# A float32 encoder layer on one core: the 1024-wide part of the input projection as seven half-size products instead of eight

## The chip, the cores and the metric

The program runs on one core of one Trainium2 chip. The metric is the device time of one execution in microseconds (us). The engines have short names: PE is TensorE (matrix products), DVE is VectorE, ACT is ScalarE, POOL is GpSimd, and SP is the engine whose queue issues nearly all DMA transfers here. Each engine works through its own instructions in order; semaphores order the engines among each other.

## What is computed

One layer (DEPTH = 1) on x of shape 1024 x 1024, all float32:

```
h = rmsnorm(x, norm1_g)
z = h @ w_in + b_in          # columns: q 512, k 128, v 128 | mq 256, mk 256, mv 512, mo 512, gates 8
att = window_sink_attention(aq, ak, av, sinks)      # 16 chunks of 64 tokens, each sees 2 chunks
mq, mk = silu(causal_dwconv([mq, mk]))              # 4 taps
ml = sigmoid(mo) * mlstm_chunkwise(mq, mk, mv, mi, mf)
x += concat(rmsnorm(att), rmsnorm per head(ml)) @ w_out
x += conv_ffn(rmsnorm(x))                           # up, 3 taps, silu gate, down
return rmsnorm(x, final_g)
```

## The kernel before

**Precision.** Every float32 factor A is split into A_hi (ACT rounds it to the type fp32r) and A_lo = A - A_hi (DVE). A product is three matmuls: hi·hi, hi·lo, lo·hi. A 128x128 by 128x512 matmul is the unit of PE's work.

**The projection.** h stands transposed in `h_hi` and `h_lo` as 8 blocks of 128 rows (k) by 1024 tokens. PE first makes the gates and column tiles 1 to 3 (their weights are split early), then "block b" for b = 4 to 10, one column tile of 128 each: `z_block(b)` is 8 k x 3 x 2 halves = 48 matmuls. Weights of tile b go through a ring of three buffers: SP loads them (`load_tile`), ACT rounds (`weight_high`, L865 to L870), DVE subtracts (`weight_low`, L1393). `z_block(b)` waits for `weight_low(b)`. DVE then takes the bank out (`z_scale`), ACT adds the bias (`z_keep`).

The remaining 1024 columns, the output gate mo and the values mv, have tokens as rows. They are the "wide" part: 16 units `wide_unit(v)` of 24 matmuls, four passes of four units, each pass 512 columns x 512 tokens over all 8 k. A pass fills four PSUM banks, which DVE takes out (`wide_keep`: times rstd, plus bias) into `ml_gate` or `ml_v`.

**Beside the blocks.** The attention runs in steps n, two per block or pair of units from block 8 on. At the even steps PE holds `turn_probs(n-2)`, `attend`, `score(n)`, `score(n+1)`, `turn_probs(n-1)`. Between a score and its turn, DVE takes the maximum (`att_top`), ACT the exponentials (`att_exps`), DVE the reciprocal of the sum (`att_sum`), POOL multiplies (`att_p_scale`, L809). `turn_values` at the start of block 8 needs `z_keep(6)`, and the first score needs `att_v_keep`. The output weights are split as the wide ones are (`wo_high`, `wo_low`), one of 8 row tiles per block from DVE's and ACT's loop index 5 on (`WO_BLOCK`), written to memory by SP (`store_wo`) and read back before the output projection.

**What sets the order.** All of it is written out by hand: a loop over `b` on ACT and DVE does in iteration b what the PE needs for block b+1 and b+2 (`weight_high(b+2)`, `z_scale(b)`, step n of the attention, taps of the convolution, `wo_*`). SP has a loop over tile numbers n from 7; in iteration n it waits until tile n-3 is used, loads tile n and does what else is attached to n. POOL has the 16 `att_p_scale` with one `decay_keep` behind each pair. SBUF is an arena of 51 slots of 4 KB per partition, with many names to one slot over time.

## Time and profile before

| | us |
|---|---|
| median of 3 runs (994.88 to 996.3) | 995.81 |
| the profiled execution | 995.28 |
| its span, first to last instruction | 993.4 |
| PE busy | 985.9 |
| DVE busy | 737.9 |
| ACT busy | 514.2 |
| POOL busy | 54.1 |

The profiled execution lies 0.5 us under the median. The span is 1.9 us shorter than that execution's own time. Busy times add up the instructions of an engine; PE's matmuls overlap, so its busy share says that there is always one in flight and not that they start as closely as they can. How closely they do is read from the distance of two starts.

### The profile page before, as it was taken

The numbers are of one execution on the slowest core, as the hardware profiler recorded it, in microseconds if no ns is written. First come the engines' busy times: TensorE is split into PE (matmuls) and PEld (weight loads), VectorE is DVE, ScalarE is ACT, GpSimd is POOL, SyncE is SP. The second block draws the span as 40 slices with busy tenths as digits, with TensorE's granted clock in tenths as the row PEclk, the third lists the DMA queues.
The fourth block names the chain that finished last, engine by engine and source line by source line (L and its number), as shares of the span: only waits on it lengthen the run. The fifth ranks groups of instructions, "written<-read, shape, count | busy, mean of one in ns | idle before, by whom it ended". The sixth has DMA issues, their size and how long they took to land.

```text
span 993.4 us, 12933 instructions
## 1 busy us (share of the span) xinstructions
PE 985.9 (99%) x4713; PEld 809.4 (81%) x4713; DVE 737.9 (74%) x1149; ACT 514.2 (52%) x1010; POOL 54.1 (5%) x53
## 2 busy tenths in 40 slices
PE   9999999999999999999999999999999999999997
PEld 7788887778888888888888888888888888888886
DVE  4563767866555669997777778777776879996896
ACT  4663556667733236654454445545445534444573
POOL 1000323311300000000000000000000000000000
PEclk9999999999999999999999999999999999999999
DMA  9528655236422242342232232223223998035104
GB/s 337 199 79 231 218 193 191 85 101 239 151 85 85 85 143 69 106 128 63 85 107 64 82 94 79 64 90 101 64 86 123 393 345 325 1 122 190 38 1 170
DMA packets 96007, 134.43 MB, mean 135 GB/s; under 512 B 6332, under 2 KB 56636, under 8 KB 95944
## 3 DMA queue, kind: packets, MB, share of 16 engines
q1 hardware_dynamic: 95128, 132.98, 40.7%
q8 instruction: 38, 0.62, 0.3%
q10 hardware_dynamic: 720, 0.61, 0.2%
q0 software_dynamic: 96, 0.00, 0.1%
q14 instruction: 25, 0.20, 0.1%
HBM read 104.75 MB, written 28.35 MB: 134 GB/s over the span
## 4 chain that ended last, share of the span: by engine, by line
PE 95%; DVE 1%; issue 1%; ACT 1%; DMA 1%; POOL 0%; SPq 0%; ACTq 0%; POOLq 0%
PE pz L2141 8%; PE pz L2434 8%; PE pz L2436 8%; PE pz L2435 8%; PE pd L2434 6%; PE pd L2436 6%; PE pd L2435 6%; PE pd L2459 4%; PE pd L2460 4%; PE pd L2457 4%; PE pz L2459 3%; PE pz L2460 3%; PE pz L2457 3%; PE pd L2335 3%; PE pd L2337 3%; PE pd L2336 3%
## 5 line engine op out<-in xcount | busy, mean ns | idle before, releaser
L1181 ACT ACTIVATE ws_hi<-raw 128x512 fp32r<-128x512 f32 x88 | 52.9, 626 | 102.5 <-PE pz L2436 47.3
L2434 PE MATMUL pz<-ht_hi,ws_hi 128*128 128x512 f32 x240 | 93.5, 390 | 0.0
L2436 PE MATMUL pz<-ht_hi,ws_lo 128*128 128x512 f32 x240 | 93.4, 389 | 0.0
L2435 PE MATMUL pz<-ht_lo,ws_hi 128*128 128x512 f32 x240 | 93.4, 389 | 0.0
L2434 PE MATMUL pd<-ht_hi,ws_hi 128*128 128x512 f32 x200 | 77.9, 389 | 0.0
L2436 PE MATMUL pd<-ht_hi,ws_lo 128*128 128x512 f32 x200 | 77.8, 389 | 0.0
L2435 PE MATMUL pd<-ht_lo,ws_hi 128*128 128x512 f32 x200 | 77.8, 389 | 0.0
L1888 DVE SCALAR_TENSOR_TENSOR gate<-u,vec,gate 128x1023 f32<-128x1023 f32 (+1 forms) x44 | 56.5, 1283 | 19.4 <-ACT gate L1223 18.6
L1858 DVE TENSOR_TENSOR ws_lo<-raw,ws_hi 128x512 fp32r<-128x512 f32 x88 | 58.6, 686 | 0.7 <-ACT ws_hi L1181 0.7
L1888 DVE SCALAR_TENSOR_TENSOR lift<-u,vec,lift 128x1023 f32<-128x1023 f32 (+1 forms) x44 | 56.2, 1278 | 0.1
L1256 ACT ACTIVATE d_hi<-a 128x512 fp32r<-128x512 f32 x44 | 27.7, 630 | 54.6 <-PE pd L2460 25.0
L2434 PEld LDWEIGHTS pz<-ht_hi,ws_hi 128*128 128x128 f32 x240 | 45.1, 188 | 9.9 <-issue 0.7
L2436 PEld LDWEIGHTS pz<-ht_hi,ws_lo 128*128 128x128 f32 x240 | 45.1, 188 | 9.4
L2435 PEld LDWEIGHTS pz<-ht_lo,ws_hi 128*128 128x128 f32 x240 | 45.0, 188 | 9.3
L1393 DVE TENSOR_TENSOR w_lo<-w_raw,w_hi 128x1024 fp32r<-128x1024 f32 x23 | 28.1, 1222 | 31.6 <-ACT w_hi L869 31.6
L2457 PE MATMUL pd<-d_hi,d_hi 128*128 128x512 f32 x132 | 51.3, 389 | 0.0
L2459 PE MATMUL pd<-d_lo,d_hi 128*128 128x512 f32 x132 | 51.3, 389 | 0.0
L2460 PE MATMUL pd<-d_hi,d_lo 128*128 128x512 f32 x132 | 51.3, 389 | 0.0
L2457 PE MATMUL pz<-d_hi,d_hi 128*128 128x512 f32 x132 | 51.3, 389 | 0.0
L2459 PE MATMUL pz<-d_lo,d_hi 128*128 128x512 f32 x132 | 51.3, 389 | 0.0
L2460 PE MATMUL pz<-d_hi,d_lo 128*128 128x512 f32 x132 | 51.3, 389 | 0.0
L2335 PE MATMUL pd<-wo_hi,mix_hi 128*128 128x512 f32 x128 | 50.9, 397 | 0.4 <-DVE mix_lo L1730 0.4
(316 smaller groups left out, 2557.4 us busy)
## 6 DMA issues: line engine op xcount, KB each, us to landing
raw<-in_w_up SPq DMA_DIRECT2D x48, 512.0 KB, 5.1
b<-in_w_down SPq DMA_DIRECT2D x49, 256.0 KB, 6.9
act_rows<-gate SPq DMA_DIRECT2D x22, 512.0 KB, 2.6
a<-act_rows SPq DMA_DIRECT2D x44, 256.0 KB, 4.7
w_raw<-in_w_wide SPq DMA_DIRECT2D x16, 512.0 KB, 3.5
x_in<-in_x SPq DMA_DIRECT2D x8, 512.0 KB, 12.9
wo_hi_rows<-wo_new_hi SPq DMA_DIRECT2D x8, 512.0 KB, 5.6
wo_lo_rows<-wo_new_lo SPq DMA_DIRECT2D x8, 512.0 KB, 6.4
```

The costliest lines, as they stand in the source:

```text
L1181: nc.scalar.activation(ws_hi[m][:, :, :], summand(p, i), ACT.Copy).then_inc(s["ws_hi_made"], 1)
L1858: nc.vector.tensor_tensor(ws_lo[m][:, :, :], summand(p, i), ws_hi[m][:, :, :].bitcast(F32), ALU.subtract)\
L1888: nc.vector.scalar_tensor_tensor(out=dst[:, back:], in0=src[:, 0:S - back], scalar=w, in1=dst[:, back:], op0=ALU.mult, op1=ALU.add).then_i ...
L2141: ins = mm(dst[:, h * HALF:(h + 1) * HALF], w[:, c], h_part(part, k, h), start=first, stop=last)
L2335: mm(bank[4 + n % 4], mix_hi[u][:, k, :], wo_hi[:, k, c], start=k == 0, stop=False)
L2336: mm(bank[4 + n % 4], mix_hi[u][:, k, :], wo_lo[:, k, c], start=False, stop=False)
L2434: mm(dst, wh[:, k, :], xh[:, k, :], start=begins and k == 0, stop=False, skip_group_check=not begins)
L2435: mm(dst, wh[:, k, :], xl[:, k, :], start=False, stop=False, skip_group_check=not begins)
L2436: ins = mm(dst, wl[:, k, :], xh[:, k, :], start=False, stop=k == KH - 1, skip_group_check=not begins)
L2457: mm(dst, d_hi[m, 0][:, c], d_hi[m, 1][:, :], start=begins and k == 0, stop=False, skip_group_check=not begins)
L2459: mm(dst, d_hi[m, 0][:, c], d_lo[m, 1][:, :], start=False, stop=False, skip_group_check=not begins)
L2460: ins = mm(dst, d_lo[m, 0][:, c], d_hi[m, 1][:, :], start=False, stop=k == KT - 1, skip_group_check=not begins)
```

## The change

The wide product W·h is cut in halves of k and of tokens, and in its two groups of 512 columns, and done with seven products of half-size matrices instead of eight. For the seven, four combinations of the halves of h and four of the quarters of the weights are needed.

- `wide_unit`: 14 units in seven products of two (`WIDE_ORDER` = 2, 5, 3, 1, 6, 7, 4). A product covers 4 k. Products 2, 5 and 1 begin the four banks anew; 3, 6, 7 and 4 add onto what the product before them left there. Each product's four banks are taken out (with the bias, or for 1, 6 and 7 onto what `ml_v` or `ml_gate` already holds), so `wide_keep` runs 28 times and not 16, and each product waits for the taking out of the one before.
- The sums of h: `load_rows` reads two 128-row blocks of x transposed, `sum_scale` (ACT, two instructions of 128x1024) applies the gain, `add_sums` (POOL, four of 128x512) makes the four combinations, `sums_high` (ACT, 128x2048) and `sums_low` (DVE, 128x2048) split them, `store_sums` (SP, two transfers of 1 MB) writes them to memory; four times (kk = 0 to 3), in two buffers. `load_sums` reads a quarter back over `h_hi` and `h_lo` before products 5, 3, 6 and 7.
- The sums of the weights: `load_weights(q)` reads four tiles of 512 KB, `add_weights(q, step)` (POOL, 128x1024) makes four, `store_weights(q)` writes them; for q = 0 and 1. They come back through the ring of tiles.
- `WO_BLOCK` is 3 and not 5: the output weights are split two iterations sooner.
- The attention keeps two steps per block through the wide part; the last steps lie closer together. `inter` and `decay` rows are spread later on SP.

The core of the diff:

```diff
-WO_BLOCK = 5
+WO_BLOCK = 3
+WIDE_ORDER = (2, 5, 3, 1, 6, 7, 4)
+UNITS = 2 * len(WIDE_ORDER)
...
@@ SP
+            def load_rows(kk):
+                ...
+                    sp.wait_ge(sum_stored[m][0], sum_stored[m][1] + 32)
+                for j in range(2):
+                    k = kk + KH * j
+                    sp.dma_start(s_sum[m][:, j, :], x_t[k * P:(k + 1) * P, :]).then_inc(sum_loaded[m][0], 16)
+            def store_sums(kk):
+                sp.wait_ge(sum_split, 2 + kk)
+                for dst, src in ((s_hi_d, s_hi), (s_lo_d, s_lo)):
+                    sp.dma_start(dst[kk], ...).then_inc(sum_stored[kk % 2][0], 16)
...
+            load_rows(0)
+            load_wo(0)
+            load_wo(1)
+            load_rows(1)
             for n in range(7, LAST_BLOCK + 1 + UNITS):
+                load_tile(n)
                 if n == 7:
-                    load_wo(0)
-                    load_wo(1)
-                load_tile(n)
+                    turn_store(0)
+                    store_sums(0)
+                    load_rows(2)
+                    store_sums(1)
+                    load_rows(3)
...
+                if n == 9:
+                    turn_store(2)
+                    store_sums(2)
+                    store_sums(3)
+                    load_weights(0)
+                    load_weights(1)
...
@@ POOL
-            for n in range(NC):
+            for kk in range(KH):
+                add_sums(kk)
+            for step in range(4):
+                add_weights(0, step)
+            att_p_scale(0)
+            add_weights(1, 0)
+            att_p_scale(1)
+            for step in range(1, 4):
+                add_weights(1, step)
+            for n in range(2, NC):
                 att_p_scale(n)
@@ ACT, iteration b, at its end
+                    if b == 3:
+                        sum_scale(half)
+                    if b == 4:
+                        sums_high(half)
+                    if b == 5 and half == 1:
+                        sum_scale(2)
+                        sum_scale(3)
+                    if b == 6:
+                        sums_high(2 + half)
@@ DVE, iteration b, at its end
+                    if half == 1 and b in (4, 6):
+                        sums_low(b - 4)
+                        sums_low(b - 3)
@@ PE
-            for v in range(UNITS):   # 16 units of 24 matmuls
+            for v in range(UNITS):   # 14 units of 24 matmuls
```

ACT's order from iteration b = 3 on. The names are `w_hi` for the rounded weights of a tile (`w_raw1` holds tile 7, `w_raw2` tile 8), `wo_new_hi` for the output weights, `z` and `zq` for what `z_keep` writes. Before:

```order
L921 ACTIVATE row_c_66<-row_c_66 4x1024
L924 ACTIVATE row_a_64<-row_b_65 4x1024
L869 ACTIVATE w_hi1_266<-w_raw1_260 128x1024
L983 ACTIVATE wo_new_hi0_57<-wo_raw0_53,vec 128x1024
L905 ACTIVATE z_59<-z_59,vec 128x1024
L869 ACTIVATE w_hi0_265<-w_raw2_261 128x1024
```

The same stretch now, tile 7 and tile 8 again the third and the last of the weights:

```order
L1095 ACTIVATE s_sum1_268<-s_sum1_268,vec 128x1024 x2
L970 ACTIVATE w_hi0_265<-w_raw0_259 128x1024
L1006 ACTIVATE zq_60<-zq_60,vec 128x16x64
...
L1025 ACTIVATE row_a_64<-row_b_65 4x1024
L1084 ACTIVATE wo_new_hi1_58<-wo_raw1_54,vec 128x1024
L1106 ACTIVATE s_hi0_271<-s_sum0_267 128x2048
L1106 ACTIVATE s_hi1_272<-s_sum1_268 128x2048
L970 ACTIVATE w_hi1_266<-w_raw1_260 128x1024
...
L1084 ACTIVATE wo_new_hi0_57<-wo_raw0_53,vec 128x1024
L1095 ACTIVATE s_sum0_267<-s_sum0_267,vec 128x1024 x2
L1095 ACTIVATE s_sum1_268<-s_sum1_268,vec 128x1024 x2
L970 ACTIVATE w_hi0_265<-w_raw2_261 128x1024
```

One output split and two splits of sums stand ahead of tile 7, and an output split and two pairs of scalings, which need newly loaded rows, ahead of tile 8.

POOL's order at the first two steps of the attention. Before:

```order
L802 MEMSET row_a_64 36x1024
L803 MEMSET row_c_66 4x1024
L809 TENSOR_TENSOR probs_312<-probs_312,inv 128x4x64
L809 TENSOR_TENSOR probs_312<-probs_312,inv 128x512
L816 AFFINE_SELECT decay_319<-decay_319 128x4x128
L809 TENSOR_TENSOR probs_312<-probs_312,inv 128x512 x2
```

Now:

```order
L910 TENSOR_TENSOR t_raw0_0_273<-t_raw0_1_274,t_raw0_0_273 128x1024
L910 TENSOR_TENSOR t_raw0_1_274<-t_raw0_2_275,t_raw0_1_274 128x1024
L910 TENSOR_TENSOR t_raw0_2_275<-t_raw0_2_275,t_raw0_0_273 128x1024
L910 TENSOR_TENSOR t_raw0_3_276<-t_raw0_3_276,t_raw0_2_275 128x1024
L879 TENSOR_TENSOR probs_326<-probs_326,inv 128x4x64
L910 TENSOR_TENSOR t_raw1_0_277<-t_raw1_1_278,t_raw1_0_277 128x1024
L879 TENSOR_TENSOR probs_326<-probs_326,inv 128x512
```

The first multiplication of the attention stands behind the 16 sums of h and the four weight sums of the first half, the second behind one more.

SP's order between tile 7 and tile 8 now (before, the loads of both tiles stood next to each other):

```order
L521 DMA w_raw1_260<-in_w_tiles 128x1024 [waits z_done]
L594 DMA wo_hi_rows<-wo_new_hi0_57 128x1024 [waits wo_split]
...
L555 DMA s_hi_rows<-s_hi0_271 128x2048 [waits x_rstd]
L555 DMA s_lo_rows<-s_lo0_269 128x2048
L550 DMA s_sum0_267<-in_x_t 128x1024 [waits x_loaded1]
...
L555 DMA s_hi_rows<-s_hi1_272 128x2048 [waits x_rstd]
L555 DMA s_lo_rows<-s_lo1_270 128x2048
L550 DMA s_sum1_268<-in_x_t 128x1024 [waits x_half_loaded]
...
L521 DMA w_raw2_261<-in_w_tiles 128x1024 [waits z_done]
```

The load of tile 8 moved behind the landing of both stores of sums (`x_loaded1` and `x_half_loaded` count them).

## Rows read from the trace of the kernel before

**Rows 1.** The page, busy time by engine.
```profile
PE 985.9 (99%) x4713; PEld 809.4 (81%) x4713; DVE 737.9 (74%) x1149; ACT 514.2 (52%) x1010; POOL 54.1 (5%) x53
```
**Rows 2.** Windows: us, busy (count) of PE PEld DVE ACT POOL; granted clock, DMA.
```profile
43.00:77.30 34.30, 34.30 (x166) 28.35 (x164) 22.45 (x25) 21.64 (x20) 0.00 (x0) 1.00 0.44 113
...
128.80:238.50 109.70, 109.63 (x602) 87.57 (x601) 77.37 (x170) 73.29 (x215) 26.42 (x17) 1.00 0.47 159
```
**Rows 3.** Timeline of PE, second and last matmul of two wide units: start, length.
```profile
142.87 0.39 PE L2369 MATMUL pz<-w_lo,h_hi 128*128 128x512 f32 x1
...
153.31 0.39 PE L2370 MATMUL pz<-w_hi,h_lo 128*128 128x512 f32 x1
```
**Rows 4.** Chain of waits: start, us, what (blocks 4 to 6, 7, turn_values, second turn_probs).
```profile
43.06 32.64 PE pz L2141 x144
...
77.34 11.11 PE pz L2141 x48
88.45 0.87 PE pd L2177 x8
...
108.52 0.59 PE pd L2204 x4
```
**Rows 5.** Timeline of ACT, iterations 3 to 6: start, us, instruction.
```profile
54.05 3.23 ACT L905 ACTIVATE zq<-zq,vec 128x1024 f32<-128x1024 f32 x3
57.19 1.04 ACT L869 ACTIVATE w_hi<-w_raw 128x1024 fp32r<-128x1024 f32 x1
...
68.20 1.06 ACT L869 ACTIVATE w_hi<-w_raw 128x1024 fp32r<-128x1024 f32 x1
...
79.28 1.15 ACT L905 ACTIVATE z<-z,vec 128x1024 f32<-128x1024 f32 x1 [1.39 <-DVE z L1427]
```
**Rows 6.** Timeline of DVE, same stretch.
```profile
59.78 1.23 DVE L1393 TENSOR_TENSOR w_lo<-w_raw,w_hi 128x1024 fp32r<-128x1024 f32 x1
...
65.87 1.21 DVE L1477 TENSOR_TENSOR row_b<-row_b,row_d 4x1024 f32<-4x1024 f32 x1
...
69.36 1.23 DVE L1393 TENSOR_TENSOR w_lo<-w_raw,w_hi 128x1024 fp32r<-128x1024 f32 x1 [1.57 <-ACT w_hi L869]
```
**Rows 7.** Groups of instructions: busy us, mean ns of one, idle before.
```profile
L1181 ACT ACTIVATE ws_hi<-raw 128x512 fp32r<-128x512 f32 x88 | 52.9, 626 | 102.5 <-PE pz L2436 47.3
...
L1858 DVE TENSOR_TENSOR ws_lo<-raw,ws_hi 128x512 fp32r<-128x512 f32 x88 | 58.6, 686 | 0.7 <-ACT ws_hi L1181 0.7
...
L1393 DVE TENSOR_TENSOR w_lo<-w_raw,w_hi 128x1024 fp32r<-128x1024 f32 x23 | 28.1, 1222 | 31.6 <-ACT w_hi L869 31.6
```
**Rows 8.** Groups of POOL, all of the span.
```profile
L829 POOL TENSOR_TENSOR mixed<-ml_t,ml_gate 128x512 f32<-128x512 f32 x8 | 10.2, 1277 | 44.0 <-DVE ml_t L1703 43.9
```
**Rows 9.** Timelines of POOL and of DVE where both read SBUF.
```profile
111.83 1.99 POOL L809 TENSOR_TENSOR probs<-probs,inv 128x512 f32<-128x512 f32 x1 [3.32 <-DVE inv L1546]
...
160.78 1.04 POOL L809 TENSOR_TENSOR probs<-probs,inv 128x512 f32<-128x512 f32 x1 [5.83 <-DVE inv L1546]
...
111.67 1.25 DVE L1567 SCALAR_TENSOR_TENSOR wo_new_lo<-wo_raw,vec,wo_new_hi 128x1024 fp32r<-128x1024 f32 x1
112.84 2.06 DVE L1493 SCALAR_TENSOR_TENSOR qk_acc<-z,vec,qk_acc 128x1022 f32<-128x1022 f32 x1
118.58 1.25 DVE L1493 SCALAR_TENSOR_TENSOR qk_acc<-z,vec,qk_acc 128x1021 f32<-128x1021 f32 x1
```
**Rows 10.** DMA: SP's issues, KB each, us to landing (128 to 140 us; all).
```profile
wo_lo_rows<-wo_new_lo SPq DMA_DIRECT2D x1, 512.0 KB, 5.9
...
act_rows<-gate SPq DMA_DIRECT2D x22, 512.0 KB, 2.6
...
w_raw<-in_w_wide SPq DMA_DIRECT2D x16, 512.0 KB, 3.5
```
**Rows 11.** GB/s in 40 slices of 92 to 104 us.
```profile
GB/s 0 0 0 0 273 410 314 219 218 259 123 68 96 191 205 273 382 423 437 423 437 369 437 437 423 396 232 0 0 0 0 0 0 177 164 410 314 246 273 205
```
**Rows 12.** Timeline of PE, its first matmuls after standing idle.
```profile
1.39 4.21 PE L2098 MATMUL pd<-idle_data 128*128 128x512 f32 x9 [1.39 <-POOL idle_data L773]
```

More of the change, by code:

```diff
@@ L994, in _ @@
                 z_keep(b)
[L995 to L996 removed]
+            for b in range(FIRST, LAST_BLOCK + UNITS // 2):
+                if 0 <= att_step(b + 1, 0) - 2 < NC - 1:
                     att_p_keep(att_step(b + 1, 0) - 2)
@@ L1029, in _ @@
                             silu_qk(n // 16 * 2 + m)
+                    if n == NC + 1:
+                        for m in range(NC - 4, NC):
+                            att_square(m)
+                    for i in DECAYS.get(n, ()):
+                        decay_exp(i)
+                    if n == NC:
+                        att_p_keep(NC - 1)
+                    if n == NC + 2:
+                        for i in range(NT // 2):
+                            wide_gate(i)
             def ml_square(i):
@@ L1084, in _ @@
             ml_key(0)
-            for i in range(NT):
+            att_total_keep()
+            for i in range(NT // 2, NT):
                 wide_gate(i)
-            att_total_keep()
             att_root()
@@ L1615, in _, with sums_low @@
             z_scale(2)
-            for b in range(FIRST, ZT + 1):
+            def sums_low(kk):
+                m = kk % 2
+                dve.wait_ge(sum_hi_made, 2 + kk)
+                nc.vector.tensor_tensor(s_lo[m][:, :, :], s_sum[m][:, :, :], s_hi[m][:, :, :].bitcast(F32),
+                                        ALU.subtract).then_inc(sum_split, 1)
+            for b in range(FIRST, LAST_BLOCK + UNITS // 2):
                 for half in range(2):
@@ L1634, in _ @@
                         z_scale(b)
-                    for m in (n - 4, n - 3):
-                        if n % 2 == 0 and 0 <= m < NC:
-                            att_keep(m)
+                    if n % 2 == 0 or n == NC + 1:
+                        first = n - 4 if n <= NC else NC - 2
+                        for m in (first, first + 1):
+                            if 0 <= m < NC and n <= NC + 1:
+                                att_keep(m)
                     if 0 <= n < NC:
```

292 lines of the change are left out of this document (197 added, 95 removed).

## The prediction, made before the changed kernel ran

> **What bounds the kernel now.** I read the page's busy times first, then the windows, then the chain of waits, then each engine's timeline from 40 to 125 us. PE is busy 985.9 of 993.4 us [rows 1] and in the wide stretch 109.63 of 109.70 us at a granted clock of 1.00, its level of 2.4 GHz [rows 2]. From 43 to 128.8 us the chain of waits is PE alone [rows 4]. So the end is set by PE: matmuls taken away count in full, and so does every wait put before PE. What must be asked of each added step is how early its result was there before. Block 7 started at 77.34 us [rows 4]; its weights were rounded by ACT from 68.20 and finished by DVE at 69.36 + 1.23 = 70.6 [rows 5, 6], 6.7 us ahead. `turn_values` started at 88.45 [rows 4]; the `z_keep(6)` that it needs ended at 79.28 + 1.15 = 80.4 [rows 5], 8.0 us ahead. These two leads are all that the new work of iterations 3 to 6 may use.
>
> **What is removed.** Two of 16 wide units, 48 matmuls. 46 starts lie between the second and the last matmul of two units: (153.31 - 142.87) / 46 = 0.227 us [rows 3]. 48 x 0.227 = **10.9 us off**, all on PE.
>
> **What a new instruction costs.** ACT: 128x1024 takes 1.05 and 128x512 0.626 [rows 5, 7], so 128x2048 takes 1.05 + 2 x 0.43 = 1.9 us. DVE: 1.222 and 0.686 [rows 7], so 2.3 us for 2048. POOL: 1.28 for 512 [rows 8]; 1.04 is the least seen [rows 9]; for 1024 I take twice that, 2.1 to 2.5. DMA: 1 MB in two stores lands 5.9 us after the second issue [rows 10], so 6.4 after the first, which SP issues some 0.5 us sooner; the engines move at most about 0.41 MB per us over a few slices [rows 11], so 2 MB land in 6.4 + 2.5 = 8.9 us; the low bound takes 2.6 us for the first 512 KB [rows 10] and gives 2.6 + 3.8 = 6.4. A lone load of 512 KB takes 3.5 [rows 10]: 1 MB 4.5 at most.
>
> **Step 1, block 7.** ACT was busy with the gates until 54 and `z_keep` until 57.2, then rounded tile 6 [rows 5]. Now an output split and four scalings of 1.05 stand ahead of that: 5.3 us later, until 63.5. DVE finishes tile 6 at 64.8; block 6 starts at 43.06 + 2 x 10.88 = 64.8 [rows 4], just in time. Everything behind is late too: DVE's tile 6 started at 59.78 [rows 6] and now at 63.6, so the gate row that ended at 65.87 + 1.21 [rows 6] ends at 70.9, ACT's second gate exponential at 72.0, the second output split at 73.1, the two splits of sums at 76.9, tile 7 at 78.0. DVE: first low part 75.0 to 77.3, second to 79.5, tile 7 at 80.8. Block 7 starts 80.8 - 77.34 = 3.5 us late. That is the short end.
> The long end adds the collisions of POOL and DVE. A POOL multiplication of 128x512 took 1.04 us at 160.78, and 1.99 at 111.83, where DVE had begun a 1.25 us instruction at 111.67; DVE's next one, at 112.84, took 2.06 and its like 1.25 at 118.58 [rows 9]. The two take turns. POOL's eight additions start at 60.4, when the first scaling is done, in the midst of DVE's gate rows; three of them fall between rows that wait for each other: 3 x 1.28 = 3.8 us. Block 7 would start at 84.7, 7.3 late.
> The Trainium skill says so too: by its page "SBUF — State Buffer", section "SBUF: two separate sides", the port pair of DVE and GpSimd is an exclusive lock held for a whole instruction, against a DVE instruction with two SBUF inputs. By that rule the long end holds; without it the short one would. The trace agrees with the lock (1.99 against 1.04).
>
> **Step 2, block 8.** The first low part is done at T0 = 77.3 to 81.1. SP then stands in one file: store both parts (8.9; low 6.4), load the next rows, store the second pair behind them (3 MB, 11.4; low 8.9), load rows 3 (4.5; low 4.0), and only behind that tile 8. Sum 24.8, low 19.3. ACT waits for those rows with two scalings ahead of tile 8: 2.1, tile 8 on ACT 1.05 and DVE 1.2, `z_scale(6)` 1.2, `z_keep(6)` 1.15: 6.7 us. So `z_keep(6)` ends at 77.3 + 19.3 + 6.7 = 103.3 at the least and 81.1 + 24.8 + 6.7 = 112.6 at the most; before it was needed at 88.45 [rows 4]. PE is **15 to 24 us late** at `turn_values`; the 3.5 to 7.3 of step 1 are in that, not beside it.
>
> **Step 3, the attention's step 2.** `turn_probs(1)`, at 108.52 before [rows 4], now stands behind POOL's weight sums. From the end of `z_keep(6)`: output split 1.05, split of sum 2 on ACT 1.9 and DVE 2.3 (5.3 in all); its store 10, since the fourth follows (low 6.4); `load_weights(0)`, 2 MB with stores in flight, 8.5 (low 7.0); four sums 10.0 (low 8.4); the first multiplication 0.6; a fifth sum 2.5 (low 2.1); the second multiplication 1.5 (low 1.04). 38.4, low 30.8. That gives 103.3 + 30.8 = 134.1 to 112.6 + 38.4 = 151.0, **25.6 to 42.5 us late**, step 2 included. I take 36, above the middle: the pair of stores and the 1.99 us are rows of this very neighbourhood, but not every wait will meet its long end. The next step of the attention finds its POOL work done in the 14 us between. From there PE's order is as before.
>
> **Clock.** Out of a long stand, PE's nine first matmuls took 4.21 us [rows 12] where nine at 0.227 take 2.0: 2.2 us. Restarts in steps 1 and 2 are hidden, since the next wait ends when the other engines say; the last one counts: +2.1. The Trainium skill, "TensorE: Matmul & The Clock Gate", section "What's actually happening", has the idle array at 1.2 GHz, half rate. The rows agree in size; a sum without the rule lacks these 2.1 us.
>
> **The wide stretch.** DVE is busy 77.37 of 109.70 us [rows 2]. It loses two weight splits and four output splits (6 x 1.2) and gains 12 `wide_keep` of 0.75; each of six product boundaries now falls behind an attention step. I take 0, with up to +6. The reload of h (2 MB) has two units and a step, 14 us, against 8.9. Behind the wide part, half the gates' sigmoids come sooner, off PE's path: 0. The earlier output splits cost nothing beyond their place in step 1, since they are needed only at the output projection.
>
> **The sum**, against the profiled execution's own 995.3 (0.5 under the median): 995.3 - 10.9 + 36 + 2.1 = 1022.5 us; the same against the median is 1023.0. I say **1022.5**.
>
> **Rivals.**
> (a) The main case, waits of 29 to 43 us: 1014 to 1029. Chance 0.50.
> (b) The short ends throughout (POOL does not hold DVE up, stores land as the fastest of before): 995.3 - 10.9 + 25.6 = 1010, with the clock 1012; 1005 to 1014. For it: 2.6 us stores are on the page [rows 10]. Chance 0.18.
> (c) DVE becomes the bound in the wide stretch besides, and the stores of 2 MB are slower than 8.9: 995.3 - 10.9 + 42.5 + 2.1 + 6 = 1035; 1029 to 1038. For it: 77.37 of 109.70, with a boundary right behind each attention step. Chance 0.13.
> (d) The weight sums are there in time after all, and only steps 1 and 2 hold: 995.3 - 10.9 + 15 to 20 = 999 to 1005. Against it: their loads cannot be issued before the third store has landed. Chance 0.07.
> (e) Other side: the file on SP, ACT and POOL stays hidden, and the 10.9 us come in full: 984.4. It decides at one place: whether `z_keep(6)` ends before PE reaches `turn_values`, near 88 us. It would need 15 us to vanish from the shortest sum above. For it: all other engines are idle much of 43 to 77 us (DVE 22.45, ACT 21.64 of 34.3, POOL 0 [rows 2]), if they overlapped better than the order lets them. Partly hidden: 984 to 994. Chance 0.09; another 0.03 for a balance near 995.
>
> **How the numbers follow.** The likeliest case is (a), 1022.5. The range 1005 to 1036 holds (a), (b) and most of (c), 0.80. A measurement of this kernel tells about 0.2% from no change. Faster than that: 0.09, (e). Within: 0.02. Slower: 0.89.
>
> **What would show it.** PE's matmuls fall by 48 and their distance stays 0.227. PE waits for the first time: at block 7 for `w_lo` (3 to 8 us), at `turn_values` or block 8 (8 to 17 us more, behind `s_sum` loads), and at the two first `turn_probs` for POOL's `probs` (10 to 20 us together). ACT's longest wait is for `s_sum<-in_x_t`. POOL's additions of 128x512 take 1.0 to 2.5 us. I am wrong if block 7 starts before 80 us, if `turn_values` starts before 100, or if the first `turn_probs` finds `probs` ready; then the sum of step 2 or 3 has a term that was hidden or a transfer that landed much sooner. If all three places hold and the time is still not within the range, the wide stretch or the output projection has changed, which the windows behind 150 us tell.

## The result: 50 us slower, and the profile after

| | before | after |
|---|---|---|
| median, us | 996.03 (4 runs, 994.88 to 996.3) | 1046.19 (4 runs, 1045.36 to 1047.62) |
| ratio | | 1.0507, 95% interval 1.0489 to 1.0526 |
| span of the profiled execution | 993.4 | 1045.9 |

The direction of the forecast was right, the size was not: 1022.5 with a range to 1036, and 1046.2 came. PE waits at the three places that the forecast names: it is 7.4 us late at the first (3.5 to 7.3 said), 22.6 at the second (15 to 24) and 45.8 at the third, 3.3 beyond its long end. And there is a fourth place, which it had priced at nothing.

The busy times of the page, for [rows 1]:

```profile
PE 987.0 (94%) x4665; PEld 808.5 (77%) x4665; DVE 764.9 (73%) x1163; ACT 528.0 (50%) x1020; POOL 96.8 (9%) x77
```

PE has 48 matmuls less and yet 1.1 us more busy time: what it saved, matmuls at half rate and slow starts after its waits take up again. Its share fell from 99% to 94%. The windows for [rows 2] (us, busy and count of PE, PEld, DVE, ACT, POOL; granted clock, DMA share, GB/s) say where:

```profile
43.00:77.30 34.30, 34.23 (x153) 27.80 (x151) 24.82 (x23) 24.53 (x22) 15.63 (x8) 1.00 0.53 157
77.30:128.80 51.50, 31.57 (x148) 25.77 (x148) 24.18 (x29) 22.16 (x28) 11.02 (x8) 0.77 0.75 271
128.80:238.50 109.70, 79.58 (x402) 62.80 (x402) 64.69 (x121) 46.76 (x145) 40.54 (x22) 0.84 0.82 292
```

PE stands 20 us in the second stretch and 30 in the third. DVE, ACT and POOL are not full in any of them; the DMA share has risen from 0.47 to 0.82 in the third. The timeline of PE gives the places (start, length, instruction, in brackets the idle time before it and what ended it). They are block 7, `turn_values`, the first score, the two first `turn_probs`, a later one, and the third wide unit (product 5, the first that needs sums):

```profile
84.76 1.19 PE L2292 MATMUL pz<-h_hi,w_hi 128*128 128x512 f32 x2 [5.90 <-DVE z L1558]
111.02 1.94 PE L2328 MATMUL pd<-ident,z 128*128 128x128 f32 x8 [12.60 <-ACT z L1006]
120.38 1.16 PE L2342 MATMUL pd<-z,zq 64*128 64x64 f32 x16 [1.42 <-ACT att_va L1060]
149.73 1.06 PE L2355 MATMUL pd<-ident,probs 128*64 128x128 f32 x4 [17.08 <-POOL probs L879]
154.34 1.12 PE L2355 MATMUL pd<-ident,probs 128*128 128x128 f32 x4 [1.54 <-POOL probs L879]
...
187.72 0.63 PE L2355 MATMUL pd<-ident,probs 128*128 128x128 f32 x4 [2.85 <-ACT probs_t L1070]
203.81 0.76 PE L2526 MATMUL pz<-w_hi,h_hi 128*128 128x512 f32 x1 [8.38 <-DVE ml_v L1734]
```

Against [rows 4], block 7 is 7.4 us late, `turn_values` 22.6, the second `turn_probs` 45.8. The wide part starts at 176.72 instead of 128.62 (timeline of PE in both), 48.1 late. Behind it come two more waits, 2.85 and 8.38, and two more stretches at the lower clock. The sum closes: 48.1 + 11.2 + 4.2 (clock, below) = 63.5; less the 10.9 us of the 48 matmuls it is 52.6, and the spans differ by 52.5.

What stands behind these waits shows in the chain of waits (start, us, what). It runs through the landings of stores that SP waits for:

```profile
80.53 5.99 DMA s_lo_rows<-s_lo
87.86 10.26 DMA s_lo_rows<-s_lo
100.59 8.31 DMA wo_lo_rows<-wo_new_lo
108.91 0.47 SPq L586
109.43 4.21 DMA wo_raw<-in_w_out
...
121.53 11.53 DMA s_lo_rows<-s_lo
135.82 12.48 DMA wo_lo_rows<-wo_new_lo
...
156.83 7.18 DMA wo_lo_rows<-wo_new_lo
...
172.51 9.32 DMA wo_lo_rows<-wo_new_lo
...
188.01 5.25 SPq L661
193.30 7.36 DMA bias_rows<-in_b_in
200.66 1.98 DVE qk_acc L1624
202.91 0.76 DVE ml_v L1734
```

Three of these landings are stores of sums. Four are `wo_lo_rows`: the output weights, which the change splits two iterations sooner and which the forecast had let pass for free. Behind the last of them come the issue and the landing of the bias, which `wide_keep` needs before the third unit can have its banks. The bias was not alone there. DVE stood idle for 9.64 us until tile weights were rounded whose load SP had issued at 185.83, behind the same landing; with its own work behind that it came to `wide_keep` at 202.64, only 0.27 us before it could begin.

The kernel's text shows one more tie. The first `wide_keep` waits until all stores of the even output tiles have landed, and the fourth for the odd ones (`dve.wait_ge(wo_stored[1], ...)`); before, only the ninth waited for them. The fourth indeed stood there (timeline of DVE):

```profile
205.62 0.75 DVE L1734 SCALAR_TENSOR_TENSOR ml_v<-pz,rstd_tok,bias_rows 128x512 f32<-128x512 f32 x1 [0.64 <-DMA wo_lo_rows<-wo_new_lo]
```

The traffic has grown too, from 134.43 MB on the page of before to

```profile
DMA packets 104551, 162.73 MB, mean 156 GB/s; under 512 B 6940, under 2 KB 57244, under 8 KB 103464
```

### The profile page after: what moved, and what is told of

Its sections match the earlier page's. It is cut to its first block, busy times and chain, and to the rows that moved or that the text cites. A ratio compares the mean times of both kernels' runs of the same rounds, so it can differ in the third digit from the quotient of the medians.

```text
span 1045.9 us, 12943 instructions
## 1 busy us (share of the span) xinstructions
PE 987.0 (94%) x4665; PEld 808.5 (77%) x4665; DVE 764.9 (73%) x1163; ACT 528.0 (50%) x1020; POOL 96.8 (9%) x77
## 2 busy tenths in 40 slices
DMA packets 104551, 162.73 MB, mean 156 GB/s; under 512 B 6940, under 2 KB 57244, under 8 KB 103464
## 4 chain that ended last, share of the span: by engine, by line
PE 80%; DMA 9%; SPq 5%; ACT 3%; DVE 2%; issue 1%; ACTq 0%
PE pz L2595 7%; PE pz L2596 7%; PE pz L2597 7%; PE pd L2595 6%; PE pd L2596 6%; PE pd L2597 6%; PE pd L2618 4%; PE pd L2621 4%; PE pd L2620 4%; DMA wo_lo_rows<-wo_new_lo 4%; PE pz L2621 3%; PE pz L2618 3%; PE pz L2620 3%; PE pd L2486 3%; PE pd L2488 3%; PE pd L2487 3%
## 5 line engine op out<-in xcount | busy, mean ns | idle before, releaser
L2526 PE MATMUL pz<-w_hi,h_hi 128*128 128x512 f32 x112 | 46.3, 414 | 8.4 <-DVE ml_v L1734 8.4
```

The lines of the kernel that those rows point to most:

```text
L2526: mm(wide_bank(t), h_hi[:, k, tok], hi[:, kk, :], start=begins and q + kk == 0, stop=False, skip_group_check=not begins)
```

## Experiments

Theory after this reading: everything is lost before the third wide unit. It is lost in files: SP stands at landings, ACT and POOL stand at operands of work that PE needs late, with work queued behind it that PE needs soon. The rivals: the seven products and their boundaries cost time themselves; the output weights are innocent; the amount (bytes, POOL's time), not the order, sets it.

### no_sums: is it the sums at all?

```diff
-            load_rows(0)
-                    store_sums(0)
-                    load_rows(2)
...
-                    load_weights(0)
-                    store_weights(0)
-                    load_sums(5)
...
-                add_sums(kk)
-                add_weights(0, step)
-                        sum_scale(half)
-                        sums_high(half)
-                        sums_low(b - 4)
...
-                        5: t_d[0, q], 6: t_d[1, q], 7: t_d[2, q], 4: t_d[3, q]}[p]
+                        5: w_wide[0, q], 6: w_wide[0, q], 7: w_wide[1, q], 4: w_wide[1, q]}[p]
```

> The changed kernel without everything that makes, stores and reloads the sums: products 5, 6, 7 and 4 take quarters of the weights and the h that is there (so the wide columns are not the reference's). The seven products, their order, the 28 takings out, the new places of the attention's last steps and WO_BLOCK = 3 all stay. Theory (the whole loss comes from the work on the sums): nothing is late, 995.8 - 10.9 = 984 to 986 us. Rival (part of the loss is in the seven products themselves, their boundaries behind an attention step, or in the output weights split two iterations sooner): 988 to 1000, with PE waiting in the wide stretch or at block 7.

Measured: 987.4 us (986.76 to 988.71) against 995.94, ratio 0.9915 [0.9901, 0.993]. That is 8.5 us less than before, of the 10.9 of 48 matmuls: a little above the 984 to 986 of the theory and just under the rival's 988. The missing 2.4 us have names: PE waits 1.64 us at the third wide unit, where DVE comes to `wide_keep` only behind an attention step, a low part and a tap of the convolution (busy from 137.36 to 144.1), and 0.6 at a `turn_probs` for a `w_lo`, whose load is on the chain there. The first is a boundary of two products, the cost that the rival names, and small. The seven products, their 28 takings out and the moved steps of the attention are thus nearly free, and the output weights two iterations sooner cost next to nothing **by themselves**.

It also places the loss. The third wide unit starts at 145.01 here and at 203.81 in the changed kernel, 58.8 us apart; the two medians are 58.8 apart too. Nothing is lost behind that unit.

### no_wo: the output weights

```diff
-            load_wo(0)
-            load_wo(1)
-                    turn_store(0)
...
-                        wo_high(b - WO_BLOCK)
-                        wo_low(b - WO_BLOCK)
```

> The changed kernel without the output weights' way: no loads, splits, stores of them beside the blocks; before the output projection the same number of bytes is read from the stored sums (the output projection multiplies by something else). Theory (the stores of the output weights, whose landing SP waits for eight times, stand in the file ahead of the sums and of the wide tiles, 5 us in step 3 and the better part of the 15 us lost behind 176 us): turn_values 1 to 3 us sooner, the second turn_probs 5 to 8 sooner, first wide unit at 168 to 172, almost no wait at unit 2; 1028 to 1038 us. Rival (the stores are absorbed in waits for the sums' own transfers): 1043 to 1047.

Measured: 1024.91 us (1023.79 to 1025.73), ratio 1.029 [1.0274, 1.0305]: 21.3 us less than the changed kernel. `turn_values` at 108.58 (2.4 sooner), the second `turn_probs` at 147.50 (6.8 sooner), first wide unit at 169.80, and no wait at the third one. Timeline of PE at the second `turn_probs`:

```profile
147.50 1.12 PE L2334 MATMUL pd<-ident,probs 128*128 128x128 f32 x4 [1.55 <-POOL probs L867]
```

The theory holds at each of its places; the time is 3.1 us below its range of 1028 to 1038, so the output weights cost more than it took. The edit removes more than stores in SP's file: eight roundings on ACT, eight low parts on DVE, 12 MB of traffic beside the blocks and the waits of `wide_keep` for the stores go with them, and no run takes these apart. Nor does any run put the output weights back to iteration 5 with the sums in place; what it costs to have them two iterations sooner, and what to have them at all beside the sums, stays open.

The time lies near my 1022.5, and that is partly chance. My sum did count two output splits in step 1, and it took 36 us at the second `turn_probs`, where this run has 39.0; with 39.0 it gives 1025.5, and 1024.9 was measured.

### tile8: the tile load behind the stores

```diff
                 if n == 7:
                     turn_store(0)
+                    load_tile(8)
                     store_sums(0)
```

> One edit: SP loads tile 8 right behind tile 7, ahead of the stores of sums. Theory (ACT stands ahead of tile 8 at the two pairs of scalings, for rows that are loaded behind the stores; the tile's own load is not the last thing): turn_values starts within 1 us of 111.0, the time stays at 1045 to 1047. Rival (the load of tile 8 behind the stores is what makes step 2 late): turn_values at 96 to 100, and 1032 to 1046 in all, as much of it as step 3 doesn't take back.

Measured: 1044.91 us (1042.37 to 1045.83), `turn_values` at 111.51. The theory holds at the place, and the time is a tenth under its range of 1045 to 1047: a load that comes in time for a step whose engine stands elsewhere brings nothing. ACT's order was the limit; it waits for the third and fourth pair of rows ahead of tile 8 (timeline of ACT in the changed kernel):

```profile
93.24 2.19 ACT L1095 ACTIVATE s_sum<-s_sum,vec 128x1024 f32<-128x1024 f32 x2 [6.41 <-DMA s_sum<-in_x_t]
103.83 2.19 ACT L1095 ACTIVATE s_sum<-s_sum,vec 128x1024 f32<-128x1024 f32 x2 [8.40 <-DMA s_sum<-in_x_t]
106.10 1.06 ACT L970 ACTIVATE w_hi<-w_raw 128x1024 fp32r<-128x1024 f32 x1
```

### pool_first: the multiplications of the attention ahead of the weight sums

```diff
-            for step in range(4):
-                add_weights(0, step)
             att_p_scale(0)
-            add_weights(1, 0)
             att_p_scale(1)
-            for step in range(1, 4):
-                add_weights(1, step)
+            for step in range(4):
+                add_weights(0, step)
+            for step in range(4):
+                add_weights(1, step)
```

> One edit: POOL's first two multiplications of the attention stand ahead of all weight sums. Theory (lateness is absorbed: behind the attention's first steps SP's own file, from the store of the first weight sums at 148.7 us to the load of tile 13 at 185.8, sets when the third wide unit can start): the second turn_probs starts near 134 and not 154, but unit 2 of the wide part starts at 198 to 203 where it started at 203.8; 1040 to 1046 us. Rival (each wait counts for itself, as the sum of my prediction has it): 18 to 20 us less, 1026 to 1029.

Measured: 1057.84 us (1056.66 to 1058.73), ratio 1.062 [1.0604, 1.0636]: **11.6 us slower** than the changed kernel. Both expectations missed. The first `turn_probs` did come at 132.48, the second at 152.39, only 2 us sooner, and it now waits on ACT. ACT's rounding of tile 10 stands ahead of the second step's exponentials, and SP had loaded tile 10 behind the eight loads for weight sums. Timelines of SP, of ACT and of POOL:

```profile
134.57 0.45 SPq L521 DMA_DIRECT2D w_raw<-in_w_tiles  x1
```
```profile
144.77 1.06 ACT L969 ACTIVATE w_hi<-w_raw 128x1024 fp32r<-128x1024 f32 x1 [17.88 <-DMA w_raw<-in_w_tiles]
```
```profile
148.58 1.99 POOL L879 TENSOR_TENSOR probs<-probs,inv 128x512 f32<-128x512 f32 x1 [19.64 <-DVE inv L1676]
150.53 21.21 POOL L910 TENSOR_TENSOR t_raw<-t_raw,t_raw 128x1024 f32<-128x1024 f32 x8
```

POOL stands 19.64 us at the second multiplication, with the weight sums, whose operands are there, queued behind it. They start at 150.53 and not at 138.53, and the third wide unit, which needs them, at 214.7 and not at 203.8. Two chains ended together at this place, 2 us apart; removing the one that showed left the other.

### both_first: both chains of step 3

```diff
                     store_sums(3)
+                    load_tile(10)
                     load_weights(0)
```

This edit stands on top of pool_first's.

> The kernel with the attention's two multiplications first on POOL, and besides the load of tile 10 ahead of the loads for the weight sums on SP. Theory (two chains ended together at step 3: POOL's weight sums, and tile 10, whose rounding stands on ACT ahead of the exponentials of the second step): now both are gone, the second turn_probs starts at 128 to 136 us where it was at 154.3 and, with POOL's alone out of the way, at 152.4; the third wide unit still starts at 195 or later, for the weight sums and SP's file; 1036 to 1048 us. Rival (a third chain is as late, or the order on POOL alone matters): the second turn_probs at 148 or later.

Measured: 1047.28 us (1046.71 to 1048.4). The time is as the theory has it, the place is not: the second `turn_probs` at 153.69, as the rival says. A third chain is as late (timeline of ACT):

```profile
151.92 1.15 ACT L1085 ACTIVATE wo_new_hi<-wo_raw,vec 128x1024 fp32r<-128x1024 f32 x1 [12.42 <-DMA wo_raw<-in_w_out]
152.97 0.57 ACT L1071 ACTIVATE probs_t<-pd 64x512 f32<-64x512 f32 x1
```

ACT stands 12.42 us at an output weight whose load SP issued at 148.57, when the store before it had landed, and the copy of the first step's probabilities is queued behind. So three chains end within 2 us of each other at the second `turn_probs`, at 154.3, 152.4 and 153.7 us. All three pass through SP's file. Each number is from another of the three kernels; but the changed kernel alone has them too: POOL's second multiplication, held up by 0.31 us for DVE's `inv` (the step whose exponentials stand behind tile 10), ends at 154.29, and ACT's copy `probs_t` at 154.04.

### wo_apart: the landing waits alone

```diff
-                    turn_store(0)
+                    store_wo(0)
                     store_sums(0)
+                    load_wo(2)
                     load_rows(2)
...
                     load_weights(0)
+                    load_wo(4)
                     load_weights(1)
...
-                    turn_store(3)
+                    store_wo(3)
                     store_weights(0)
+                    load_wo(5)
```

> The changed kernel; SP no longer waits for a store of output weights to land right behind issuing it: the reload of the raw buffer (load_wo) is issued later in SP's file, behind other work. Same transfers, same work on all engines. Theory (the output weights cost 21 us through SP's waits): the second turn_probs moves by less than 3 us from 154.3, since both chains that end there stay; the loads of tiles 12 and 13 are issued 8 to 15 us sooner against the second turn_probs, the wait at the third wide unit (8.4 us) falls under 3; 1030 to 1038 us. Rival (the DMA engines are full there, and it is the traffic of the output weights that costs): tile 13 lands no sooner; 1042 to 1047.

Measured: 1040.61 us (1039.54 to 1041.35), ratio 1.0449: 5.6 us less. In the wide stretch the theory holds. The wait at the third unit falls from 8.38 to 0.87 us, and from the second `turn_probs` to that unit it is 38.5 us and not 49.5. That unit starts at 198.03, 5.8 sooner, which is the whole gain; the other 5.2 us of the 11.0 make up for the later `turn_probs`, and how much of them is only lateness that a wait took up is not shown. But at step 3 my new order cost 5.2 us: `load_wo(4)`, between the two loads of weights, waits for a landing itself and holds tile 10 up, so the second `turn_probs` came at 159.57, where the theory allowed 3 us. The range of 1030 to 1038 was missed by that.

### no_pool: POOL's additions

```diff
-                add_sums(kk)
-                add_weights(0, step)
...
-                act.wait_ge(pool_summed, POOL_SUMMED + 4 * (kk + 1))
+                act.wait_ge(sum_scaled, 2 + kk)
```

> The changed kernel without POOL's 24 additions (sums are what was loaded and scaled; all transfers, scalings and splits stay). Theory (POOL and DVE hold each other up over SBUF, and this makes the difference between my short and my long end of step 1): block 7 starts at 80.5 to 82 us where it started at 84.8, turn_values at 103 to 106 (111.0); the second turn_probs 8 to 14 us sooner, bounded by the load of tile 10 behind the weight loads; 1030 to 1040 us. Rival (no such collisions, block 7 is late through ACT's and DVE's own new work): block 7 at 84 to 85, turn_values 3 to 5 sooner only, 1038 to 1044.

Measured: 1043.22 us (1043.15 to 1043.88), block 7 at 81.25 us (84.76), `turn_values` at 107.90, second `turn_probs` at 151.30. Step 1 is settled: 81.25 lies where the short end (80.8) was, 84.76 where the long end (84.7) was, and what lies between them is POOL beside DVE. ACT did not wait for POOL's results there: its splits of sums follow its output split at once in both kernels. It is DVE's gate rows that are stretched. One tiny instruction of DVE, of 4x7 elements, shows it, in the timelines of before, of the changed kernel and of this one:

```profile
64.43 0.16 DVE L1472 TENSOR_TENSOR m_prev<-row_b,row_d 4x7 f32<-4x7 f32 x1
```
```profile
68.12 1.08 DVE L1603 TENSOR_TENSOR m_prev<-row_b,row_d 4x7 f32<-4x7 f32 x1
```
```profile
67.57 0.16 DVE L1596 TENSOR_TENSOR m_prev<-row_b,row_d 4x7 f32<-4x7 f32 x1
```

In all it brought 3 us and not 6 to 16; `turn_values`, 3.1 us sooner, and the time lie where the rival had them. At step 3 ACT stands 19.33 us at tile 10 and 2.15 at an output weight, and they hold PE up all the same.

### thin: the bytes

```diff
-                    sp.dma_start(dst[kk], src[kk % 2][:, :, :].rearrange("p j n -> p (j n)").bitcast(F32))
+                    sp.dma_start(dst[kk][:, 0:256], src[kk % 2][:, 0, 0:256].bitcast(F32))
...
-                    sp.dma_start(dst, t_raw[q][j][:, :])
+                    sp.dma_start(dst[:, 0:128], t_raw[q][j][:, 0:128])
```

> The changed kernel with the same number of transfers in the same order, but the stores of both kinds of sums and the reload of h move an eighth of their bytes, and products 5, 6, 7 and 4 take quarters of the weights as they are (some 21 MB less moved; what is computed in the wide columns is not the reference's). Loads of x, of the weights and the way of the output weights stay whole. Theory (what SP waits for is the landing of large transfers, so the bytes give the length of the file): turn_values at 97 to 103 us (111.0), second turn_probs at 128 to 140 (154.3), no wait worth 3 us at the third wide unit; 1012 to 1026 us. Rival (the order in the file and the instructions on the engines set the times, the bytes hardly matter): second turn_probs at 148 or later, 1036 or more.

Measured: 1023.07 us (1021.39 to 1023.49), ratio 1.027 [1.0252, 1.0287]: 23.1 us less with the same number of transfers in the same order. By the pages it moved 18.35 MB less (162.73 - 144.38), not 21. `turn_values` at 102.39, second `turn_probs` at 138.22; at the third wide unit PE still waits 3.90 us, where the theory allowed less than 3. The landing of the first pair of stores fell from 6 us to 2.1, and from 10.3 to 5.0 for the second. The theory holds but for that wait: a good part of the length of SP's file is made of bytes. What is left in its chain of waits are output weights, and the wait at the third unit (last line, timeline of PE) hangs on a load of wide weights that takes 10.41 us to land:

```profile
90.95 8.60 DMA wo_lo_rows<-wo_new_lo
...
120.44 11.65 DMA wo_lo_rows<-wo_new_lo
```
```profile
178.71 0.76 PE L2526 MATMUL pz<-w_hi,h_hi 128*128 128x512 f32 x1 [3.90 <-DVE ml_v L1734]
```

### woven: another order, weight sums first

```diff
-            load_rows(0)
+            load_weights(0)
             load_wo(0)
             load_wo(1)
-            load_rows(1)
+            load_weights(1)
...
+            for q in range(2):
+                for step in range(4):
+                    add_weights(q, step)
+            for kk in range(3):
+                add_sums(kk)
             att_p_scale(0)
             att_p_scale(1)
+            add_sums(3)
```

> The seven products with the same sums, instructions and bytes in another order: weight sums first (loaded from 43 us on, before the sums of h), the four sums of h spread over iterations 5 to 8 in three buffers (the third in the slots of the gate rows), tile loads never behind a landing that is later than they are, store_wo and load_wo apart, the bias ahead of the reload of h, the attention's two first multiplications behind three of four sums of h. Theory (the loss lies in the order: work whose result is needed late stands ahead of work that is needed soon): PE waits at most a few us in all; 985 to 1000 us. Rival (the loss lies in the amount: 28 MB more to move and POOL's 43 us beside DVE): 1010 or more.

Measured: 1031.92 us (1030.47 to 1032.76), ratio 1.036 [1.0344, 1.0375]: 14.3 us less than the changed kernel, but on the rival's side, though with my fault in it (below) it does not decide between the two. Two waits of PE make most of it, 10.25 us at block 6 and 14.40 at a later `turn_probs`. The second is a fault of mine: the ninth `z_scale` waits for the last store of sums, because its row lies in a slot of that buffer. The first is the same hold-up as in step 1, much stronger. Timelines of POOL and of DVE:

```profile
54.33 26.82 POOL L920 TENSOR_TENSOR t_raw<-t_raw,t_raw 128x1024 f32<-128x1024 f32 x8 [13.83 <-DMA t_raw<-in_w_wide]
```
```profile
55.30 4.39 DVE L1604 TENSOR_TENSOR_SCAN row_d<-reset,row_b 4x1024 f32<-4x1024 f32 x1
59.73 2.70 DVE L1605 COPY row_b<-row_d 4x1024 f32<-4x1024 f32 x1
62.47 3.29 DVE L1607 TENSOR_TENSOR row_a<-row_a,row_b 4x1024 f32<-4x1024 f32 x1
65.79 2.19 DVE L1608 COPY row_c<-row_b 4x7 f32<-4x7 f32 x1
```

Before, these four took 2.28, 0.68, 1.21 and 0.16 us. Each is longer by 2.0 to 2.1, which is about one POOL addition of 128x1024 (2.4 us alone, 9.59 / 4 in the changed kernel), and POOL's own took 26.82 / 8 = 3.35 on the average.

### eased: the order that the runs point to

```diff
+        s_sum = [at(n, f"s_sum{m}", [2, S]) for m, n in enumerate((24, 43, 30))]
...
+            for kk in range(3):
+                add_sums(kk)
+            att_p_scale(0)
+            add_sums(3)
+            att_p_scale(1)
+            for q in range(2):
+                for u in range(2):
+                    add_weights(q, 2 * u)
+                    add_weights(q, 2 * u + 1)
+                    att_p_scale(2 + 2 * q + u)
...
+                    if b == 5 and half == 1:
+                        sums_high(1)
+                    if b == 6 and half == 0:
+                        sum_scale(2)
+                    if b == 7:
+                        if half:
+                            sum_scale(3)
+                        else:
+                            sums_high(2)
+                    if b == 8 and half == 0:
+                        sums_high(3)
```

> All of the change's sums and bytes, placed by what the runs so far showed: sums of h first and sums of the weights last; a third buffer for sums in the slots of the gate rows, so that the third pair of rows does not wait for a store to land; the rounding of tiles 7 and 8 ahead of sums on ACT; one pair of scalings or one split per iteration, behind what PE waits for; weight sums in two buffers of slots that are free by then (not the one that the ninth z_scale needs), and between POOL's multiplications two additions at a time; tile loads ahead of loads for weight sums, store_wo and load_wo apart, bias ahead of the reload of h. Theory (the loss lies in the order of work on SP, ACT and POOL): the waits at block 7, turn_values, the first two turn_probs and the third wide unit are together under 12 us, and the time is 988 to 1003 us. Rival (with this much to move and to add, no order hides it: DMA engines and the hold-ups between POOL and DVE set it): 1010 or more.

Measured: 1025.49 us (1023.96 to 1026.32), ratio 1.0291 [1.0275, 1.0306]: 20.7 us less than the changed kernel with all of its sums and bytes. The order helped at the three first places: block 7 at 80.18, `turn_values` at 92.78 (111.02), second `turn_probs` at 123.47 (154.34). The theory misses all the same, in the time and in the waits: at its places they are 1.24, 0, 1.30, 4.96 and 6.82, in all 14.3 us and not under 12, and there are others between (2.89, 5.97). The second `turn_probs` is still 15 us later than before the change, the first wide unit comes at 153.16 and the third at 174.19. The windows from 80 us on:

```profile
80.00:100.00 20.00, 19.09 (x80) 15.40 (x80) 11.03 (x16) 11.24 (x11) 1.76 (x2) 0.91 1.01 374
100.00:120.00 20.00, 14.29 (x84) 11.32 (x84) 13.69 (x20) 11.14 (x26) 12.01 (x8) 0.95 1.02 410
120.00:140.00 20.00, 16.45 (x80) 12.90 (x80) 18.19 (x17) 8.08 (x24) 18.09 (x9) 0.79 0.93 329
140.00:160.00 20.00, 14.10 (x64) 11.41 (x64) 15.29 (x21) 9.88 (x28) 13.36 (x6) 0.83 0.97 344
160.00:180.00 20.00, 13.18 (x63) 10.43 (x60) 10.94 (x23) 3.93 (x14) 1.99 (x1) 0.83 1.03 400
```

The last but one column, the DMA share, is 0.93 to 1.03 for 100 us; DVE and POOL are at 18 of 20 us from 120 to 140. A better order brought the transfers nearer to each other until they filled the DMA engines. The time is on the rival's side; that the amount is what is left is read from these shares, and the next two runs test it.

### eased_thin and eased_no_wo: do the causes add up?

The edits are those of thin and of no_wo, on top of eased.

> The reordered kernel eased with the stores of both kinds of sums and the reload of h at an eighth of their bytes, as in thin (wide columns not the reference's). Theory (two causes that add up: where work stands in each engine's file, and the DMA engines, which in eased are busy 0.93 to 1.03 of the time from 80 to 180 us so that every landing takes 8 to 13 us): each alone gave 21 to 23 us of 50; together the loss is nearly gone, 990 to 1002 us, first wide unit at 136 to 144. Rival (both remove the same waits): 1012 or more.

Measured: 1005.46 us (1004.29 to 1006.4), ratio 1.0096: 20.0 us less than eased, 3.5 us above what the theory allows. The two gains nearly add up: 40.7 us together, 20.7 and 23.1 alone. Most waits are gone or short (1.24, 2.84, 3.17, 0.87, 2.80, 1.39 us); the larger ones end at `probs_t` and `ml_v`, that is at ACT and DVE. That POOL beside them is the reason was not tested here.

> The reordered kernel eased without the output weights' way beside the blocks, as in no_wo (the output projection multiplies by something else): 4 MB of loads and 8 MB of stores less between 43 and 190 us, and 8 roundings and 8 low parts less on ACT and DVE. Theory (the DMA engines are the bound in eased): these 12 MB are 29 us of DMA time at 0.41 MB per us; 993 to 1006 us, with the DMA share under 0.9 in most of 80 to 180 us. Rival (the bound is POOL with DVE and ACT, not the DMA engines): 1012 or more.

Measured: 1000.46 us (1000.09 to 1001.05), ratio 1.0048 [1.0032, 1.0065]: 25.0 us less than eased. The time lies in the theory's range, its mark for the DMA engines doesn't hold: they are still at 1.01, 0.99, 0.97 and 0.88 from 80 to 160 us, only PE hardly waits for them. A share near 1 is thus no proof by itself that the DMA engines hold PE up; that their bytes cost time is shown by the two runs with fewer bytes. The largest wait left is theirs: the last store of weight sums takes 12.76 us to land, and the tile load behind it makes PE wait 5.20 us (chain of waits):

```profile
143.27 12.76 DMA t_rows<-t_raw
156.05 3.64 DMA w_raw<-t_rows
159.71 1.06 ACT w_hi L965
160.80 1.23 DVE w_lo L1519
162.08 1.11 PE pd L2348 x4
```

In one line, all medians in us: changed 1046.2; output weights away 1024.9; fewer bytes 1023.1; better order 1025.5; better order and fewer bytes 1005.5; better order and output weights away 1000.5; no sums at all 987.4; before 996.0. No version with all of the work beat the kernel before.

## Why the prediction was right and wrong

**What bounds the kernel, and what is removed.** Right. 48 matmuls fewer; no_sums gives 8.5 of the 10.9 us, with 2.3 us of small waits beside it.

**What a new instruction costs.** Right, but for one addition. ACT 128x2048 takes 1.81 to 1.91 us (1.9 said), DVE 2.25 (4.49 for two; 2.3 said), POOL 128x1024 2.40 (2.1 to 2.5), 128x512 1.26 to 2.18 and once 3.25 (1.0 to 2.5). The first pair of stores landed 6.4 us after its first issue, my low bound; the second pair 10.7, where I had 11.4.

**Step 1.** Right at its long end, 84.76 for 84.7, and for its reason: without POOL's additions it is 81.25, so they cost 3.5 us where I took 3.8. That the sum came out to a tenth is luck. PE did not wait for tile 7's low part, which ended at 83.48, 1.2 sooner than I had it, but for `z_scale(5)` behind it on DVE, 1.1 us that my sum lacks. The sentence of the Trainium skill that I had weighed there ("SBUF — State Buffer", section "SBUF: two separate sides": an exclusive lock held for a whole instruction) is borne out by the 4x7 instruction `m_prev`, which takes 0.16 us alone and 1.08 beside POOL.

**Step 2.** Right in time, 22.6 us late with 15 to 24 said, `z_keep(6)` ending at 110.8 with 103.3 to 112.6 said. One part of the reason was wrong: I let tile 8 wait for the stores, but with that load moved ahead of them (tile8) nothing changes. It is the scalings that stand ahead of it on ACT, and they wait for rows that SP loads behind the stores; that part I had.

**Step 3.** Too small: 45.8 us late where I took 36, and 3.3 above my long end. From the end of `z_keep(6)` it took 43.6 us and not at most 38.4. Three terms grew. ACT's output split had to wait 2.90 us for its raw rows, whose load SP issued when the store before had landed; the loads for weight sums took 12.1 us to land, not 8.5, beside output weights; and POOL's two multiplications took 1.59 and 1.99 us, not 0.6 and 1.5. The store of sums was shorter than I had it, 7.5 us for 10. Without output weights the place comes at 147.50, 39 us late, within my range. I had listed one chain to this place. There were three, and the other two were as late. The signs that I had listed say so too: ACT's longest wait before the wide part is not for `s_sum` (8.40 us) but for tile 10, 18.91 us, and tile 10 stands behind the loads for weight sums on SP.

**Clock.** Right for the one restart that I counted: 45.8 us late at `turn_probs`, 48.1 at the first wide unit, 2.3 more with a wait of 0.27 in it. But there were two further waits in the wide part, and a restart behind each. Two rows of PE's timeline behind the last of them, and the window of that stretch, with a granted clock of 0.50, the level of 1.2 GHz:

```profile
204.37 0.63 PE L2528 MATMUL pz<-w_lo,h_hi 128*128 128x512 f32 x1
204.79 0.63 PE L2530 MATMUL pz<-w_hi,h_lo 128*128 128x512 f32 x1
```
```profile
203.80:209.50 5.70, 5.70 (x14) 4.44 (x15) 3.70 (x10) 1.44 (x4) 0.00 (x0) 0.50 0.98 331
```

Starts lie 0.427 us apart and not 0.227. 13 of them cost 2.6 us here, and 8 cost 1.6 at 189 to 192.

**The wide stretch, and "the earlier output splits cost nothing". This is the step that failed.** I gave it 0 to 6 us, and it took 15.4: waits of 2.85 and 8.38, and 4.2 of clock. My reason for 0 was that the output weights are needed only at the output projection. That is when they are needed, not what they hold up; and the first `wide_keep` waits for their stores. These are 8 MB, and SP waits for a landing before it loads the next raw tile. The 5.9 us of [rows 10] is one landing of eight: before, they took 4.1 to 15.0 us, 6.4 in the median, and none held PE up. Now they take 3.6 to 12.5, 7.7 in the median, but the four from the one at 135.82 on take 12.5, 7.2, 9.3 and 9.9, with wide tiles, the bias and the reload of h behind them. no_wo prices all that belongs to the output weights at 21.3 us (6.8 by the second `turn_probs`, the rest behind it); in no_sums, where they stay and the sums go, only 2.4 us are missing. It is the meeting of the two that costs, and I had priced each by itself. How much of the 21.3 is SP's waiting, how much traffic and how much work on ACT and DVE is open; wo_apart, which moves only the landing waits, gains 5.6, with 5.2 lost at step 3 by its own order. With step 3 and the wide stretch as measured the sum is 995.3 - 10.9 + 45.8 + 2.1 + 15.4 = 1047.7, and the profiled execution took 1047.6: 9.8 us were missing in step 3 and 15.4 in the wide stretch.

**The rivals.** None reaches the time; the highest, (c), ends at 1038. (a) and (b) had the right places, (c) the right direction, but the wrong engine: before the third unit DVE stood idle for 9.64 us, waiting for tile weights. It was SP's file. The forecast's last sentence, that a time outside the range with all three places in order means the wide stretch, is half of what happened: the wide stretch it was, but the third place was 3.3 us beyond its long end too.

## What to carry to other kernels

Work that is "needed only much later" isn't free: look at what it holds up in the queue of the engine that issues it, and count every landing that this queue waits for, old ones too, and not at the length of one quiet row. When several chains pass through one queue, expect them to end together; pool_first took away the one that showed and lost 11.6 us. And a move that saves 1% of PE's work and adds 28 MB (162.73 - 134.43) of traffic must be set against the DMA engines stretch by stretch, not against their mean share.

## What the runs showed that I had not expected

- A DVE instruction of 28 elements costs as much as POOL's instruction beside it: `m_prev` (4x7) took 0.16 us alone, 1.08 beside additions of 128x512 and 2.15 beside additions of 128x1024 (in woven). In a row of small dependent instructions every one pays. Each such row lost about 1 us beside the short additions and 2 beside the long ones; whether the same work in shorter additions would cost less in all was not tried.
- The landing of the same transfer differs widely within one kernel. 1 MB of output weights in two stores lands 4.1 to 15.0 us after the second issue before the change, and 3.6 to 12.5 after it; the 15.0 falls in a stretch before the change where the DMA share is 0.96 to 1.00 (70 to 90 us). One row is no price for all of them.
- What is still open: the 13 us between eased_no_wo (1000.5) and no_sums (987.4). The trace names waits of 5.20, 3.35, 0.75 and 0.61 us and the clock behind the two longer ones; no run takes them apart.
